# Four U tiles run before the first V stage, and ScalarE builds the plain one-hot vectors, in an encoder layer with a product-key expert layer

## The reference

```python
q = (xt @ w_pq).reshape(T, PEER_HEADS, PEER_QUERY)
s1 = jnp.einsum('thd,nd->thn', q[..., :PEER_HALF], sub_keys1)
s2 = jnp.einsum('thd,nd->thn', q[..., PEER_HALF:], sub_keys2)
v1, i1 = lax.top_k(s1, 16)
v2, i2 = lax.top_k(s2, 16)
# 256 sums v1 + v2, the best 16 of them: idx = i1 * 128 + i2, gate = softmax
act = gelu(einsum('thkd,td->thk', peer_u[idx], x)) * gate
out = einsum('thk,thkd->td', act, peer_v[idx])
```

## Time and profile before

| | |
|---|---|
| median of 3 runs | 3187.49 us (3186.56 to 3188.06) |
| the profiled execution | 3188.36 us, its span 3186.5 us |
| TensorE busy | 3082.0 us, 97% |
| VectorE busy | 2062.2 us, 65% |
| ScalarE busy | 364.4 us, 11% |
| GpSimd busy | 696.4 us, 22% |
| mean granted TensorE clock | 0.989 of full speed |
| HBM traffic | 1000.79 MB read, 20.97 MB written |

### The profile page before, as it was taken

The page is one execution under the profiler, slowest core; times in us unless marked ns, Lnnn a source line. Parts: engine busy times, 40 slices in busy tenths (PEclk is TensorE's granted clock), DMA queues, the critical chain, the costliest instruction groups (busy, mean ns, idle before and its releaser), DMA issues.

```text
span 3186.5 us, 26888 instructions
## 1 busy us (share of the span) xinstructions
PE 3082.0 (97%) x10342; PEld 1885.6 (59%) x10342; DVE 2062.2 (65%) x3070; ACT 364.4 (11%) x650; POOL 696.4 (22%) x553
## 2 busy tenths in 40 slices
PE   8999999999996999999989999999999999999997
PEld 5444444444445478679873446885448884468743
DVE  5364633442777798999996766656566565555575
ACT  1223202311001211112210000000000000000000
POOL 0000000000331143422224343223222222222230
PEclk9999999999997999999999999999999999999998
DMA  7222221176896698999999999999999999999995
GB/s 276 73 79 72 82 66 60 37 265 237 317 411 278 259 387 353 422 394 370 380 359 384 399 392 421 421 418 417 418 421 421 418 419 416 422 421 421 418 406 217
DMA packets 151655, 1023.44 MB, mean 321 GB/s; under 512 B 16368, under 2 KB 21616, under 8 KB 35568
## 3 DMA queue, kind: packets, MB, share of 16 engines
q0 software_dynamic: 78800, 559.97, 42.9%
q1 hardware_dynamic: 72736, 461.86, 37.0%
HBM read 1000.79 MB, written 20.97 MB: 321 GB/s over the span
## 4 chain that ended last, share of the span: by engine, by line
DMA 39%; PE 36%; DVE 18%; issue 4%; POOL 1%; ACT 1%; DVEq 0%; SPq 0%; ACTq 0%
DMA arena<-peer_v,arena 37%; PE ps L726 11%; DVE arena L1909 6%; PE ps L1170 5%; PE ps L996 3%; PE ps L1143 3%; PE ps L894 2%; PE ps L920 2%; DVE arena L1950 2%; DVE arena L1898 2%; PE ps L797 1%; DVE arena L1947 1%; DVE arena L1836 1%; DMA arena<-peer_ut 1%; PE ps L690 1%
## 5 line engine op out<-in xcount | busy, mean ns | idle before, releaser
L1170 PE MATMUL ps<-arena 128*128 128x512 f32 x2048 | 884.1, 594 | 18.4 <-DVE arena L1961 14.2
L1143 PE MATMUL ps<-arena 128*128 128x256 f32 x4096 | 892.6, 379 | 2.4 <-DMA arena<-peer_ut 2.4
L1143 PEld LDWEIGHTS ps<-arena 128*128 128x128 f32 x4096 | 774.6, 190 | 110.5 <-DMA arena<-peer_ut 4.6
L1909 DVE SCALAR_TENSOR_TENSOR arena<-arena 128x2048 f32<-128x2048 f32 x256 | 602.9, 2355 | 296.3 <-DMA arena<-peer_v,arena 229.6
L1898 DVE CUSTOM_DVE_ANT_0 arena<-arena 128x2048 f32<-128x2048 f32 x256 | 587.0, 2294 | 276.6 <-DMA arena<-peer_u,arena 275.9
L1170 PEld LDWEIGHTS ps<-arena 128*128 128x128 f32 x2048 | 390.1, 191 | 510.1 <-issue 488.4
L638 POOL DMA_INDIRECT arena<-peer_u,arena x256 | 347.5, 1357 | 1060.9 <-DVE arena L1898 864.5
L653 POOL DMA_INDIRECT arena<-peer_v,arena x256 | 325.5, 1272 | 722.9 <-DVE arena L1909 682.4
L726 PE MATMUL ps<-arena 128*128 128x512 f32 x800 | 345.2, 592 | 1.1 <-ACT arena L1210 1.1
L726 PEld LDWEIGHTS ps<-arena 128*128 128x128 f32 x800 | 151.9, 190 | 192.2 <-issue 192.2
L1210 ACT ACTIVATE arena<-ps 128x512 f32<-128x512 f32 (+2 forms) x247 | 144.5, 612 | 763.6 <-PE ps L912 147.4
(11 more groups left out here) (183 smaller groups left out, 1847.9 us busy)
## 6 DMA issues: line engine op xcount, KB each, us to landing
arena<-peer_ut SPq DMA_DIRECT2D x128, 1024.0 KB, 9.2
arena<-peer_vt SPq DMA_DIRECT2D x128, 1024.0 KB, 9.1
arena<-w_row SPq DMA_DIRECT2D x52, 1024.0 KB, 8.3
arena<-w_mix SPq DMA_DIRECT2D x40, 1024.0 KB, 4.9
arena<-w_once SPq DMA_DIRECT2D x74, 512.0 KB, 3.5
arena<-w_feat SPq DMA_DIRECT2D x20, 1024.0 KB, 10.0
dense_gates<-arena SPq DMA_DIRECT2D x8, 2048.0 KB, 8.6
arena<-dense_gates POOLq DMA_DIRECT2D x11, 1024.0 KB, 24.5
```

The lines of the kernel that those rows point to most:

```text
L1143: last = pe.matmul(ps[:, (e // 2) % 4, (e % 2) * DT:(e % 2 + 1) * DT], w[:, kt * P:(kt + 1) * P], XTD[:, kt * DT:(kt + 1) * DT], start=(kt ...
L1170: last = pe.matmul(bank(4 + (c % 2) * 2 + tb), G[:, t * DT + tb * P:t * DT + (tb + 1) * P], w[:, i * 512:(i + 1) * 512], start=(t == 0), s ...
L1909: dve.scalar_tensor_tensor(out=acc, in0=VB[e], scalar=AV[r // 4 % 2][:, r % 4:r % 4 + 1], in1=acc, op0=ALU.mult, op1=ALU.add).then_inc(v_f ...
```

## The change

1. Four U tiles of group 1 run right after group 0's U tiles, ahead of its V quads, on every engine's list; the first five weighs stand at positions 0, 0, 4, 5, 8 instead of 0, 1, 2, 3, 5 (where positions 0 to 3 are now those four tiles).
2. The plain one-hot vector moves to ScalarE, as Abs(t - iota) four times, and Relu(1 - that) once, in `plain_vectors`, called one group ahead of `stage_gates`. TensorE waits for it too (`plain_ready`).
3. VectorE does a whole row after every third group of the one-hot stretch (20 rows) instead of one per four groups in two halves (16 rows). Of the rows between the mixing sums four go (6 + 6 become 4 + 4), and two come behind the probabilities of blocks 2 and 3. Before the group stages 78 rows are done, not 76. Gelus of rows move later on ScalarE.
4. In the last column the four last quads run first for block 2, then for block 3, and VectorE adds, norms and stores block 2 by itself before block 3.

```diff
+U_AHEAD = 4
-HALVES_BEFORE = 38
+HALVES_BEFORE = 39
...
+W_UNITS += [f"U1.{_t}" for _t in range(U_AHEAD)]
...
-        return (0, 1, 2, 3, 5)[q]
+        return (0, 0, 4, 5, 8)[q]
...
-GELU_AT = [16 * k + 8 for k in range(4)]
+HOT_ROWS = [3 * i + 2 for i in range(20)]
+GELU_AT = [HOT_ROWS[4 * k + 3] + 2 for k in range(5)]
...
-                if p == TILES[0] + 6:
+                if p == TILES[0] + 8:
                     load_gates(4)
...
             def one_hots(first, count):
                 for n in range(first, first + count):
                     pe.wait_ge(hots_ready, n + 1)
+                    pe.wait_ge(plain_ready, n + 1)
...
+            def last_quads():
...
+                for tb in range(DB):
+                    for l in range(n - SLOTS, n):
...
+                    if tb == 0:
+                        last.then_inc(first_sum, 1)
...
+            for t in range(U_AHEAD):
+                u_tile(1, t)
...
+            def plain_vectors(n):
+                if n >= 2:
+                    act.wait_ge(oh_mm, n - 1)
+                if n:
+                    act.wait_ge(plain_ready, n)
+                for i in range(4):
+                    t = DT + 4 * n + i
+                    last = act.activation(FAR[:, i * NK:(i + 1) * NK], IOTA, ACT.Abs, scale=-1.0, bias=TB[:, t:t + 1])
+                last.then_inc(far_done, 1)
+                act.wait_ge(far_done, n + 1)
+                act.activation(OH[n % 2][:, 4 * NK:8 * NK], FAR, ACT.Relu, scale=-1.0, bias=ONES[:, 0:1]
+                               ).then_inc(plain_ready, 1)
...
+            plain_vectors(0)
             for n in range(DT // 4):
+                if n + 1 < DT // 4:
+                    plain_vectors(n + 1)
                 if n % 8 == 1:
...
-                dve.tensor_tensor(oh[:, 1], IOTA.unsqueeze(1).broadcast_to([P, 4, NK]),
-                                  turn[:, 1, here].unsqueeze(2).broadcast_to([P, 4, NK]), ALU.is_equal)
...
             some_rows(2)
             for k, b in enumerate((2, 3, 1)):
                 add_mix(b, 2, k, "mix231.2")
-            some_rows(6)
+            some_rows(4)
...
-            some_rows(6)
+            some_rows(4)
             for k, b in enumerate((3, 1)):
                 add_mix(b, 1, k, "mix31.1")
...
+            some_rows(2)
             best_keys(3, "b0.key3")
...
                 one_hot_vectors(n)
-                if n % 4 == 1:
-                    row_ahead(rows[0])
-                if n % 4 == 3:
-                    row_add(rows[0])
-                    rows[0] += 1
+                if n in HOT_ROWS:
+                    some_rows(1)
```

More of the change, by code:

```diff
@@ L1570, in rows_until @@
                     gate_exps(12 + ROUTE_POS[p])
-            p = 0
+            for p in range(U_AHEAD):
+                rows_until(p)
+            p = U_AHEAD
             for g in range(4):
@@ L2085, in rows_until, with last_stats @@
                     gates(12 + ROUTE_POS[p - 3], 1, ROUTE_POS[p - 3])
-            def last_stats(c):
-                for tb in range(DB):
+            def last_stats(c, blocks=range(DB)):
+                for tb in blocks:
                     dve.wait_ge(x_added, 24 + 2 * c + tb + 1)
@@ L2091, in last_stats @@
                 return last
-            p = 0
+            for p in range(U_AHEAD):
+                for q in range(TILES[0] // 8):
+                    if weigh_pos(q) == p:
+                        weigh(q, q)
+                rows_until(p)
+            p = U_AHEAD
             for g in range(4):
```

88 lines of the change are left out of this document (59 added, 29 removed).

## The result

The changed kernel takes 3234.07 us (median of 4 runs, 3228.97 to 3236.62), the kernel before 3187.69 in the same comparison: a ratio of 1.0144, 95% interval 1.0127 to 1.0162. It is slower, as forecast, but by 46 us instead of 13, and outside the range.

A forecast was written before the change was run, and what follows sets the result against it. The prediction took TensorE, busy in 97% of the span, and its waits as the bound. Its terms, +18.7 + 2 - 0.95 - 6.3 = +13.4 us on a profiled 3188.36, gave 3201, put at 3200 (8 in 10: 3162 to 3220).

The forecast's parts named there:

- half clock and last weigh: After the ninth V quad: about 2 us at half clock, and the 0.95 us wait for the last weigh goes.
- Row order: Ahead of the one-hot stretch: four rows fewer before the last mixing sum remove TensorE's waits, -31.5 us (-22 to -33).
- ScalarE's chain: One-hot stretch: plain vectors queue behind ScalarE's store wait, stopping TensorE; seven cycles, +51 us (+30 to +72).
- the cycle of eight groups: One-hot stretch: 8.5 us of store, 18.3 of ScalarE work, about 2 waiting for TensorE: 29 us against 21.7.
- signs named ahead: One-hot stretch: seven TensorE waits of 4 us or more for the Relu; ScalarE idle about 8.5 us before every eighth eviction.
- The rival of gathers: ScalarE's wait stays hidden; gathers bound the stretch, 23.3 us per eight groups, +11 us, total 3163; chance 0.19.
- The fifth weigh: First V stage: twelve rows ahead of it take 86 us (74 to 92), so TensorE waits 20 us before the ninth quad.
- Early U tiles: First V stage: four U1 tiles add 27.6 us of cover, so its waits and their half clocks go.
- Split end: End of the kernel: only one block's work is left after TensorE's end, 9.3 us, not 15.6: -6.3 us.
- The first: Rival: ScalarE's wait stays hidden and gathers bound the one-hot stretch, +11 us, total 3163; chance 0.19.
- second: Rival, first V stage: gathers run faster and the fifth weigh is in time, -8.3 us, total 3179; chance 0.13.
- The third: Rival, one-hot stretch: cycles of 32 us, +72 us there, +34.5 in all, total 3222; chance 0.13.

The follow-up runs named there:

- rows16: The changed kernel with 16 rows in halves in the stretch, not 20 whole, and row Gelus behind groups 16k + 15: stretch 224.7 us, total 3214.37 us.
- gelu_only: The changed kernel with each row Gelu on ScalarE one group earlier, two of them thus ahead of the store wait: stretch 248.1 us, total 3222.81 us.
- vector_gelu: The changed kernel with plain vectors made on VectorE again and row Gelus one group earlier: stretch 210.7 us, total 3186.21 us.
- weigh_early: The changed kernel with third to fifth weighs at tiles 2, 4, 6, not 4, 5, 8, and the fifth's gates loaded two tiles earlier: 3225.31 us.

## Why the prediction was right and wrong

Its terms against the trace, as shifts of TensorE's timeline:

| step | predicted | measured |
|---|---|---|
| start of the stretch | -30.5 | -31.85 |
| length of the stretch | +51 | +89.9 |
| ninth V quad | +18.7, behind a wait of 20 | +53.2, behind 14.5 |
| half clock and last weigh | +1.05 | +0.8 |
| end | -6.3 | -6.1 |
| sum | +13.4 | +48.0 |

**Row order: right.** 31.85 us, and the transposes behind `b0.pq2` wait for nothing. That these 31.5 us would stand in the total is partly luck: it held because the stretch then made TensorE late. On its own the row order is worth 16.5.

**The stretch: the chain was right, and the step that failed is the one put at nothing.** The sum gave the stretch +51 for ScalarE's chain, and nothing for the rows: "20 rows instead of 16: 64 x 1.03 + 20 x 4.6 = 158 us against 177. It no longer sets the pace" looked at VectorE's time alone. The runs show 54.0 us for the chain alone, near the 51, and 35.9 us more (rows16 against the changed kernel) for what the 20 rows bring with them. Of those 35.9 the place of the row Gelus, behind the store wait, is 12.5, as gelu_only has it; "hidden under the waits of ScalarE" was said of the Gelus ahead of the stretch, and not asked within it. The other 23 us, by subtraction, belong to four more rows and to whole rows in one piece. No run parts these two. What the traces show of them: 20 rows keep the transfers busy for an estimated 192 us instead of 170, stores land 12.0 us after issue (median in the stretch) against 7.3 in rows16, and a whole row makes TensorE wait for scaled vectors and then run slower (vector_gelu).

In the forecast's own terms the cycle of eight groups is 29 us; the six cycles between ScalarE's first and last waiting eviction (1448.26 and 1657.78) are 34.9 on average. From a store's issue to the next eviction 11.1 us pass (mean of seven), not 8.5, and ScalarE waits 5.3 us per cycle for TensorE, not 2 (31.6 us over these cycles): together the 5.9 us per cycle that were missing. 24 us of the 90 are slower matmuls, where the upper bound had 2 us per cycle. With 16 rows in halves and the Gelus away from the store the cycle is 28.9 us, which is the forecast's 29, though with a shorter store and a longer wait for TensorE than it took. Of the signs named ahead, seven waits of 4 us and more for the Relu, four came (8.8, 9.1, 4.9 and 8.2 us); the other three are 2.5 to 3.6 us. ScalarE's idle before every eighth eviction is 9.2 us on average, not 8.5.

**The rival of gathers was underpriced.** "23.3 us per eight groups at 420 GB/s" took the rate of one full window. Over a stretch with stores and gathers the rate is 369 to 388 GB/s at a DMA share of 0.94 to 0.98 (five kernels), so the transfers of 20 rows are busy for about 192 us, not 186, and the stretch was never shorter than 204.

**The fifth weigh: right.** Its rows take 86.5 us less weighs (1721.9 to 1812.95, less two weighs of 2.28), predicted 86. TensorE came 5 us later relative to VectorE than forecast, so waited 14.5 and not 20. Placing the weigh earlier removes it, as weigh_early shows.

**Early U tiles**: with them alone the 17 us of waits in the first V stage go, as forecast, and the total gains 4.3 us, since a wait of 16.5 us for a tile Gelu, queued behind Gelus of rows, takes their place. **Split end: right**, 12.7 us from the last matmul to the end, predicted 12.5.

**The rivals.** The first and second are ruled out by the seven stalls and the wait for the fifth weigh. The third, longer cycles of 32 us by slower stores and half clock, has the right direction and names two of the causes, not the row Gelus or the rows. It is still 3 us per cycle short.

By the Trainium skill (ScalarE: Activation LUTs, "What ACT_TABLE_LOAD costs") an Abs over 128 elements is an estimated 387 ns and a Relu over 512 an estimated 707; the trace has 390 and 722 and so agrees. Neither is where the time went.

## What to carry to other kernels

When work moves to an idle engine, read that engine's queue and not its busy share: everything behind its longest wait is moved behind that wait too, and here it was two things, plain vectors and row Gelus, of which each stopped TensorE by its own path. Putting the needed items ahead of the wait gives back 54 of the 90 us (260.6 to 206.5 us with two edits that change no work). And a time computed for one engine alone, as the 158 us of VectorE here, says nothing of the order in which others wait for its pieces. Before counting a removed wait as won, ask what comes late next: of 31.5 and 17 us of waits removed only 16.5 and 4.3 stayed, and later waits for weighs and Gelus, both queued behind rows, grew in their place. Behind the stretch rows wait for gathers while the transfers run at a share of 0.97 to 1.01; that the full transfers are what keeps the rows from catching up is read from the traces, and no run varied them there.

## What the runs showed of the hardware

TensorE ran slower behind some waits as short as 2.7 us. Behind each of the ten such waits in vector_gelu's stretch the next 24 matmul records took 6.4 to 6.5 us instead of 4.67, and the mean granted clock there is 0.92; the changed kernel, with waits of up to 9.1 us, has 0.84. But behind a wait of 3.15 us at 1469.54 in the changed kernel eight records took 1.16 us and the half U tile its usual 3.62, so the length of the wait alone does not decide. The 16 DMA engines held 419 GB/s at a share of 1.01 over 315 us with gathers and loads alone, and 369 to 388 at 0.94 to 0.98 where 2 MB stores run among them. A store of 2 MB landed 7.3 to 9.5 us after its issue (medians of eight stores, in nine kernels) with 16 rows in the stretch, and 8.9 to 10.6 (nine kernels) with 20.
